# One-pass spread of the norm factors, wide-wide-low-low matmuls, and an earlier emptying of a short projection step in a fused two-block kernel

## The reference, cut to what matters

```python
def first_block(x, ...):                      # 256 tokens, D = 2048
    z = rmsnorm(x, norm_mix) @ w_in           # parts: hq hf hi hgate aq ak av g_hg g_at
    o_hg = rmsnorm(hgrn2(hq, hf, hi), hg_norm) * silu(hgate)      # 8 heads of 128
    qa, ka = rmsnorm(aq, q_norm), rmsnorm(ak, k_norm)             # heads of 64
    mixed = sigmoid(g_hg) * (o_hg @ w_hg_out) + sigmoid(g_at) * (swa_sinks(qa, ka, av) @ w_at_out)
    x = x + mixed @ w_out
    return x + square(relu(rmsnorm(x, norm_ffn) @ w_up)) @ w_down
def second_block(x, ...):
    proj = (rms_norm(x) * (1 + scale_a) + shift_a) @ w_in_2       # c drives scale, shift, gate
    diff_out = rms_norm(differential_attention(...), g_diff_sub)  # 8 heads of 128
    dsa_out = indexed_sparse_attention(...)
    x = x + gate_a * rms_norm(concat(diff_out, dsa_out) @ w_o)
    return x + gate_f * rms_norm((silu(h @ w_gate) * (h @ w_up)) @ w_down)
```

## Time and profile before

| | us |
|---|---|
| median of 3 runs | 2599.99 (2598.31 to 2602.0) |
| profiled execution, its own time | 2600.71 |
| its span in the trace | 2598.9 |
| PE busy in the span | 2545.6 (98%) |
| DVE busy | 1802.2 (69%) |
| ACT busy | 1254.9 (48%) |

### The profile page before, as it was taken

The page is one execution under the profiler, slowest core; times in us unless marked ns, Lnnn a source line. Parts: engine busy times, 40 slices in busy tenths (PEclk is TensorE's granted clock), DMA queues, the critical chain, the costliest instruction groups (busy, mean ns, idle before and its releaser), DMA issues.

```text
span 2598.9 us, 36089 instructions
## 1 busy us (share of the span) xinstructions
PE 2545.6 (98%) x14646; PEld 2214.9 (85%) x14646; DVE 1802.2 (69%) x2496; ACT 1254.9 (48%) x1868; POOL 0.2 (0%) x4
## 2 busy tenths in 40 slices
PE   7999999999999999999999999999799999999998
PEld 6888899988888888888887899987688888888886
DVE  5557547578878788788788767775766646665555
ACT  5456436455544344444444444565544444443453
POOL 0000000000000000000000000000000000000000
PEclk8999999999999999999999999999899999999999
DMA  7655444788878878879879454545477667657553
GB/s 255 199 180 169 149 146 132 248 296 280 290 237 276 295 251 309 288 259 317 277 264 326 152 178 159 151 163 183 161 240 231 224 209 227 227 192 207 185 179 129
DMA packets 349773, 574.47 MB, mean 221 GB/s; under 512 B 29414, under 2 KB 174080, under 8 KB 348712
## 3 DMA queue, kind: packets, MB, share of 16 engines
q1 hardware_dynamic: 300912, 450.53, 53.3%
q10 hardware_dynamic: 48696, 121.65, 13.4%
HBM read 560.31 MB, written 10.70 MB: 220 GB/s over the span
## 4 chain that ended last, share of the span: by engine, by line
PE 95%; DVE 2%; ACT 1%; issue 1%; DMA 0%; ACTq 0%; DVEq 0%
PE ps L453 33%; PE ps L454 17%; PE ps L476 9%; PE ps L478 9%; PE ps L477 9%; PE ps L737 3%; PE ps L957 2%; PE ps L738 2%; PE ps L739 2%; PE ps L958 2%; PE ps L959 2%; DVE wl L1702 1%; PE ps L821 1%; PE ps L542 0%; ACT wh L1031 0%
## 5 line engine op out<-in xcount | busy, mean ns | idle before, releaser
L1702 DVE TENSOR_TENSOR wl<-raw,wh 128x1024 fp32r<-128x1024 f32 x856 | 1041.1, 1224 | 749.1 <-ACT wh L1031 745.9
L1031 ACT ACTIVATE wh<-raw 128x1024 fp32r<-128x1024 f32 x856 | 900.8, 1060 | 1137.2 <-PE ps L454 555.8
L453 PE MATMUL ps<-hs,wh 128*128 128x512 f32 x3536 | 1250.3, 398 | 5.3 <-DVE hs L1888 2.9
L454 PE MATMUL ps<-hs,wl 128*128 128x256 f32 x3536 | 993.8, 281 | 0.0
L453 PEld LDWEIGHTS ps<-hs,wh 128*128 128x128 f32 x3536 | 665.2, 188 | 169.0 <-issue 3.9
L454 PEld LDWEIGHTS ps<-hs,wl 128*128 128x128 f32 x3536 | 669.4, 189 | 0.2
L476 PE MATMUL ps<-wh,ff 128*128 128x512 f32 x864 | 336.6, 390 | 0.0
L478 PE MATMUL ps<-wh,ff 128*128 128x512 f32 x864 | 336.2, 389 | 0.0
L477 PE MATMUL ps<-wl,ff 128*128 128x512 f32 x864 | 336.2, 389 | 0.0
L476 PEld LDWEIGHTS ps<-wh,ff 128*128 128x128 f32 x864 | 162.2, 188 | 33.8
L478 PEld LDWEIGHTS ps<-wh,ff 128*128 128x128 f32 x864 | 162.2, 188 | 33.7
(11 more groups left out here) (295 smaller groups left out, 2196.0 us busy)
## 6 DMA issues: line engine op xcount, KB each, us to landing
raw<-w_down SPq DMA_DIRECT2D x108, 1024.0 KB
raw<-w_in SPq DMA_DIRECT2D x80, 1024.0 KB
raw<-w_up SPq DMA_DIRECT2D x64, 1024.0 KB
ada_w<-w_ada ACTq DMA_DIRECT2D x96, 512.0 KB, 5.5
ada_more<-w_ada ACTq DMA_DIRECT2D x96, 512.0 KB, 6.5
raw<-w_gate SPq DMA_DIRECT2D x88, 512.0 KB
raw<-w_up SPq DMA_DIRECT2D x88, 512.0 KB
raw<-w_in SPq DMA_DIRECT2D x72, 512.0 KB
```

The source lines that it names most:

```text
L453: nc.tensor.matmul(ps[0:m, b, :], wh[:, slot, w0:w0 + m], x2, start=k == 0, stop=False)
L454: mm = nc.tensor.matmul(ps[0:m, b, 0:T], wl[:, slot, w0:w0 + m], x2[:, 0:T], start=False, stop=end)
L1031: nc.scalar.activation(wh[:, h % WH_SLOTS, :], raw[:, slot, HALF * q:HALF * (q + 1)], ACT.Copy).then_inc(wh_ready, 1)
L1702: nc.vector.tensor_tensor(wl[:, h % WH_SLOTS, :], raw[:, slot, HALF * q:HALF * (q + 1)], wh[:, h % WH_SLOTS, :], ALU.subtract).then_inc(wl ...
```

## The change

1. In a wide step the two pairs of a tile are written wide, wide, low, low.
2. `spread` becomes fp32r with 52 rows (rows 0 to 19 and the same again in rows 32 to 51), and the moving tile `factors` (52 x 256, fp32r) holds the high part of the factors in rows 0 to 19 and the rest in rows 32 to 51. `pair_invert` makes it with two more DVE operations, each after the one before. Since fp32r is made by an engine's write, `spread` is loaded to a side tile and copied by ACT (two copies, later one).
3. ACT and DVE empty step 10 before the `feed` of half panel 91. The first half panel of the first gate step takes its tiles in the order 2, 3, 0, 1, and waits for step 10's sums only ahead of tiles 0 and 1.
4. For PN_DIFF the squares of the last pair, its sums, the roots and the inversion move forward by one n, the spreads and the scaling from n = 101 to 100, and `attention_high` starts pair by pair; `attention_low` stands at n = 100 too.

```diff
-        spread = at("spread", [20, 20 * 64], F32, 181)
+        spread = at("spread", [52, 20 * 64], F32R, 181)
...
+        factors = at("factors", [52, T], F32R, 206)
...
                         for kk in range(2):
                             k = 2 * h + kk
-                            end = k == 4 * panels - 1
-                            x2 = rhs(n, k)
                             w0 = 512 * kk + c0
-                            nc.tensor.matmul(ps[0:m, b, :], wh[:, slot, w0:w0 + m], x2, start=k == 0, stop=False)
-                            mm = nc.tensor.matmul(ps[0:m, b, 0:T], wl[:, slot, w0:w0 + m], x2[:, 0:T],
-                                                  start=False, stop=end)
+                            nc.tensor.matmul(ps[0:m, b, :], wh[:, slot, w0:w0 + m], rhs(n, k), start=k == 0, stop=False)
+                        for kk in range(2):
+                            k = 2 * h + kk
+                            w0 = 512 * kk + c0
+                            mm = nc.tensor.matmul(ps[0:m, b, 0:T], wl[:, slot, w0:w0 + m], rhs(n, k)[:, 0:T],
+                                                  start=False, stop=k == 4 * panels - 1)
...
-                                              spread[:, c:c + P], rstd[0:20, 1, :], start=True, stop=True)
+                                              spread[:, c:c + P], factors[:], start=True, stop=True)
...
-                    for n, (c0, m) in enumerate(FULL):
+                    for n in (2, 3, 0, 1) if (s, h) == (0, 0) else range(4):
+                        c0, m = FULL[n]
                         if h == 0 and s == 0:
-                            pe.wait_ge(tile_summed, 4 * LY.step + (8 if n else 5))
+                            pe.wait_ge(tile_summed, 4 * LY.step + (5, 8, 4, 4)[n])
...
-                if n == 99:
+                if n == 98:
                     pair_sums(PN_DIFF, 4, part=PN_DIFF[3:4])
-                if n == 101:
-                    pe.wait_ge(sem("spread_loaded"), 32)
+                if n == 100:
+                    pe.wait_ge(sem("spread_loaded"), 3)
                     pair_spreads(PN_DIFF, (5, 6, 7, 4))
...
+                    if (s, h) == (10, 7):
+                        copy_halves(10, 0, 44, 0, widths=(P, P))
                     feed(8 * s + h + 4, 0)
...
+                    if (s, h) == (10, 6):
+                        act.wait_ge(sem("spread_in"), 32)
+                        for part, cols_ in spread_in:
+                            nc.scalar.activation(spread[:, cols_], part[:], ACT.Copy
+                                                 ).then_inc(sem("spread_loaded"), 1)
...
-                if n in (88, 92, 96, 98):
+                if n in (88, 92, 96, 97):
...
-                if n == 99:
+                if n == 98:
                     pair_roots(PN_DIFF, 4)
-                if n == 101:
-                    act.wait_ge(sem("pair_normed"), 13)
-                    attention_high(range(8, ND))
+                if n == 100:
+                    for j in range(4):
+                        act.wait_ge(sem("pair_normed"), 10 + j)
+                        attention_high((8 + 2 * j, 9 + 2 * j))
...
-                nc.vector.reciprocal(rstd[0:20, 1, :], rstd[0:20, 1, :]).then_inc(sem("set_inverted"), 1)
+
+                link(nc.vector.reciprocal(rstd[0:20, 1, :], rstd[0:20, 1, :]))
+                link(nc.vector.tensor_copy(factors[0:20, :], rstd[0:20, 1, :]))
+                nc.vector.tensor_tensor(factors[32:52, :], rstd[0:20, 1, :], factors[0:20, :], ALU.subtract
+                                        ).then_inc(sem("set_inverted"), 1)
...
+                    if (s, h) == (10, 7):
+                        total(10, 0, 0, z[:, Z_AK_RAW, :])
+                        total(10, 0, 1, z[:, Z_AV, :], inc=3)
                     feed(8 * s + h + 4, 0)
...
-                if n == 99:
+                if n == 98:
                     pair_invert(PN_DIFF)
-                if n == 101:
+                if n == 100:
                     pair_scale(PN_DIFF, (5, 6, 7, 4))
-                if n == 102:
-                    attention_low(range(8, 12))
-                if n == 103:
-                    attention_low(range(12, ND))
+                    attention_low(range(8, ND))
```

More of the change, by code:

```diff
@@ L168, in build @@
         sel = at("sel", [P, 2, 38], F32, 199.5)
-        spread = at("spread", [20, 20 * 64], F32, 181)
+        spread = at("spread", [52, 20 * 64], F32R, 181)
+        spread_in = [(at("spread_in0", [52, 1024], F32, 168), slice(0, 1024)),
+                     (at("spread_in1", [52, 256], F32, 122.5), slice(1024, 1280))]
+        spread_in2 = at("spread_in2", [52, 1280], F32, 156)
         psq = at("psq", [P, 2, 2, T], F32, 188)
@@ L694, in heads_of_first @@
                 if n == 0:
-                    pe.wait_ge(sem("spread_loaded"), 16)
+                    pe.wait_ge(sem("spread_loaded"), 2)
                     pair_spreads(PN_Q, (4, 5, 6, 7))
@@ L1261, in _ @@
             for s in range(6, 11):
-                halves = 8
-                for h in range(halves):
+                for h in range(8):
+                    if (s, h) == (10, 7):
+                        copy_halves(10, 0, 44, 0, widths=(P, P))
                     feed(8 * s + h + 4, 0)
@@ L1278, in _ @@
                         act.wait_ge(sem("trig_made"), 6)
-                        act.dma_start(spread[:], k_spread).then_inc(sem("spread_loaded"), 16)
+                        for part, cols_ in spread_in:
+                            act.dma_start(part[:], k_spread[:, cols_]).then_inc(sem("spread_in"), 16)
                         act.wait_ge(tile_summed, 4 * 9 + 12)
                         pair_squares(PN_Q[:2])
+                    if (s, h) == (10, 6):
+                        act.wait_ge(sem("spread_in"), 32)
+                        for part, cols_ in spread_in:
+                            nc.scalar.activation(spread[:, cols_], part[:], ACT.Copy
+                                                 ).then_inc(sem("spread_loaded"), 1)
                     if (s, h) == (10, 3):
@@ L1284, in _ @@
                         pair_roots(PN_Q, 4)
-                copy_halves(s, 0, 4 * s + 4, 0, widths=(P,) * (4 if s < 10 else 2))
+                if s < 10:
+                    copy_halves(s, 0, 4 * s + 4, 0)
             def keys_out(t0, n, count, b):
@@ L1568, in heads_of_second @@
                     act.wait_ge(sem("rope_sin"), 18)
-                    act.dma_start(spread[:], k_spread).then_inc(sem("spread_loaded"), 16)
+                    act.dma_start(spread_in2[:], k_spread).then_inc(sem("spread_in"), 16)
+                if n == 90:
+                    act.wait_ge(sem("spread_in"), 48)
+                    nc.scalar.activation(spread[:], spread_in2[:], ACT.Copy).then_inc(sem("spread_loaded"), 1)
                 if n - 7 in DIFF_UNITS:
@@ L1579, in heads_of_second @@
                     diff_values(3)
-                if n in (88, 92, 96, 98):
-                    j = (88, 92, 96, 98).index(n)
+                if n in (88, 92, 96, 97):
+                    j = (88, 92, 96, 97).index(n)
                     act.wait_ge(DIFF["out_hi"], 2 * j + 2)
@@ L2017, in _ @@
                         hg_products(h - 3)
+                    if (s, h) == (9, 0):
+                        link(nc.vector.memset(factors[:].bitcast(F32), 0.0))
                     if (s, h) == (10, 4):
                         pair_invert(PN_Q)
-                for n in range(4 if s < 10 else 2):
-                    total(s, 0, n, z[:, 4 * s + n if s < 10 else (Z_AK_RAW, Z_AV)[n], :],
-                          inc=3 if (s, n) == (10, 1) else 1)
+                if s < 10:
+                    to_z(0, s, s)
             def hg_mask(h):
@@ L2498, in constants @@
         k_dup=np.stack([(p[:, None] == 64 * h + p[None, :] % 64) for h in range(2)], axis=1).astype(f32),
-        k_sel=sel, k_spread=(np.arange(20)[:, None] == np.arange(20 * 64)[None, :] // 64).astype(f32),
+        k_sel=sel, k_spread=((np.arange(52)[:, None] % 32) == np.arange(20 * 64)[None, :] // 64).astype(f32),
         k_rot=rot, k_invf=invf, k_alibi=alibi, k_causal=causal,
```

## The result

The changed kernel took 2570.99 us (median of 4 runs, 2569.97 to 2572.05) against 2600.99 for the kernel before beside it: a ratio of 0.9882, 95% interval 0.9871 to 0.9894. The forecast was 2574 with 2561 to 2590. The profiled execution took 2572.05 us, its span is 2570.2, that is 28.7 less than the span before; the medians lie 30.0 apart.

What follows compares the result with a forecast made beforehand. PE, busy 2545.6 of 2598.9 us, was taken to set the time. Terms of 10 + 9.3 - 0.3 + 2.3 + 3.2 + 1.3 = 25.8 us off the median 2599.99 gave 2574 us, range 2561 to 2590.

Steps and rivals of the forecast that it cites:

- the order: Wide steps: wide, wide, low, low makes slow groups of four 6.6 ns shorter, quick ones unchanged; 10 us saved.
- the spreads: Spread products of PN_Q, PN_HG and PN_DIFF: 26 one-pass fp32r matmuls replace 52 records; 9.3 us saved.
- the gate start: First gate step: PE runs tiles 2 and 3 while DVE's totals are awaited; 2.3 us saved.
- The -0.3 us for the squares of PN_Q: One more DMA issue ahead of these squares may make PE wait about 0.3 us longer; bounds 0 and -0.6.
- Rival (c): Wide steps: two lows in a row leave only 0.120 us for each weight load, so slower; 2622 us, chance 0.06.
- Rival (a): Wide steps: the order makes no difference, a low beside a wide costs what it costs; 2584 us, chance 0.25.
- 26 fp32r matmuls of 256 columns at 0.120: Time of all spread products after the change: 3.1 us, against 12.0 us plus 0.4 before.
- the branch for which I had 1.6: First gate step: if the clock still falls at about 269.6 us, 1.6 us are saved, against 3.05 without a fall.
- The half clock at PN_HG: From 385.6 to 392.4 us: no clock fall expected with a block of 1 us; 3.2 us saved, bounds 0 and 3.2.
- PN_DIFF: Norm moved earlier: PE's stop ahead of L8B goes, 1.3 us saved.
- parts 2 and 5: The one-pass spread products, 9.3 us saved, and the earlier PN_DIFF removing the stop ahead of L8B, 1.3 us saved.

Runs made afterwards that it cites:

- run 3: Changed kernel with every second tile of a half panel, except in a step's first half panel, written low, low, wide, wide; 2578.54 us.
- run 9: Changed kernel in the old order, with 64 of 128 weight columns in every wide matmul of a wide step but a sum's first; 2550.49 us, one run.
- run 10: Changed kernel in the old order, with 64 weight columns in the low matmuls, all but the first and last of a sum; 2569.95 us, one run.
- run 2: Changed kernel with the old order wide, low, wide, low put back; 2584.22 us, ratio 0.9928.
- Run 7: Changed kernel with the spread matrix and the factors padded from 52 to 128 rows; 2570.99 us.
- run 11: Changed kernel once more, without further edit, to stand on one chip with a later version; 2569.57 us, ratio 0.9885.
- run 1: Kernel before with only the wide steps written wide, wide, low, low; 2589.85 us, ratio 0.9954.
- run 5: Kernel before with the moves alone (step 10 emptied first, tile order, PN_DIFF one n sooner), plain fp32 spreads, old order; 2598.3 us, ratio 0.9985.
- run 4: Kernel before with the one-pass spread alone (fp32r, 52 rows, factors in two parts); 2592.49 us, ratio 0.9965.
- run 6: Changed kernel with DVE's inversion of the PN_Q factors and ACT's two spread copies put behind the emptying of step 10; 2570.94 us.
- run 8: Changed kernel with spread padded to 128 rows, ACT's copies late, and DVE's step 10 totals ahead of the feeds of half panels 89, 90, 91; 2567.61 us, ratio 0.9869.

## Why the prediction held, point by point

The total came within 3 us of the forecast, and part of that is luck: the order brought 3.8 us more than I had, the spreads and the gate start 2.0 less. The -0.3 us for the squares of PN_Q didn't come; PE's short wait between their sums is 0.20 us before and 0.17 after.

**1. The order: the sign was right, the size 13.8 instead of 10, and the reason wrong.** I had each change of width cost the same. Run 3 has little more than half the changes and is 7.5 us slower, so that is not it. The neighbours don't cost what I took from steps of one width either: in the changed trace wide after wide takes 232.9 ns, low after low 114.6, and the two other distances 349.2 together, where I had 227, 120 and 353.3. Runs 9 and 10 show that the excess depends on the number of weight columns. That it is the loading of them, and not the writing of as many output rows, is argued: no run changes one without the other. With 64 columns in the wide, loaded while a low runs, a pair takes 0.340 us, 0.680 a group (run 9). Against that, 128 columns everywhere have an excess of 13 ns a group in the quick spacing, 27 in the slow one, and 17 in the new order. The slow spacing needs 128 columns on both sides, since it goes when either is halved (one execution each). The new order never shows it; for that it gives up the quick one, 0.697 against 0.693. So slow groups gained 10 ns, not 6.6, and quick ones lost 3.3, where I had them unchanged. 0.79 x 1896 x 10 - 0.21 x 1896 x 3.3 is 13.7 us, and the trace has 13.8. Rival (c), too little room in a row of lows, was refused for two lows by this result. For four, run 3 shows its size, 4 ns a group: a low takes 118.3 ns there in the mean and 115.3 in the changed kernel, and the wides no more than before.

The Trainium skill, TensorE: Matmul & The Clock Gate, section "LDWEIGHTS (loading the stationary operand)", gives a load of P columns P / 1.2 ns, that is 107 ns for 128 columns and 53 for 64. At the 2.4 GHz of the same page a stream of 256 columns takes 107 ns too; that is an estimate. So a low would only just cover a full load, and a wide would cover it with ease. Run 9 agrees with this; run 10 does not, since a shorter load under the wide should have changed nothing and took away the slow spacing.

The Trainium skill, TensorE: Matmul & The Clock Gate, section "Back-to-back issue gap", says that in a stream of weight loads and matmuls both set the distance between matmuls. Runs 9 and 10 agree in kind; its figure for 512 columns, 131 ns, is not what the across steps show, 227. Rival (a), that the order makes no difference, had the changed kernel at 2584 us; it came out at 2571, and the same kernel in the old order (run 2) at 2584.

What stays open is why the old order has two spacings, and what puts a stretch into one of them. It isn't the kind of spread (run 2), and it differs between runs of one kernel.

**2. The spreads: 9.3 us forecast, 7.9 measured.** The count and the 3.65 us were right. The step that was off is "26 fp32r matmuls of 256 columns at 0.120": a block of eight takes 1.14 and a block of two 0.43, 3.85 us in all instead of 3.1. The longer distance behind a block stays (0.4 us in all), and 0.25 went to the half clock at the first block. Run 7 names the reason, the 52 rows of weights between matmuls of 128; I had written that the rows change nothing that the trace shows, which was so only because no row of before had a one-pass matmul of few rows. DVE's two operations took 0.28 and 0.41 us, and from the first of them to the `feed` behind them it takes 0.76, against 0.9.

**3. The gate start: 2.3 us forecast, 1.7 measured.** The stop was 2.00 us against 2.05, in the place forecast, and the clock fell: the branch for which I had 1.6. A stop of 1.9 to 2.1 us stands there in seven traces: behind it the clock fell in four (the changed kernel and runs 2, 9 and 10) and not in three (3, 7 and 11). Behind the stop near 616 us it fell in the traces of before and of runs 1, 3, 6 and 9 and not in the others. A single execution has the one or the other, so taking the middle was fair, and what decides stays open.

**4. The half clock at PN_HG: 3.2 us forecast, 3.1 measured.** The kernel before and runs 1 and 5 have plain fp32 spreads and all show it; the changed kernel and the ten other runs have one-pass spreads and none does. I had written that it depended on where the block came, because the same block at the two other places was followed by no fall. That was wrong: in run 5 the clock fell at both. So the long block brings the fall on here in three traces of three and at each of the two other places in one of three; why not always stays open.

**5. PN_DIFF: 1.3 us forecast, 1.5 measured.** The sum was right and the split between parts 2 and 5 was not: run 4 shows that without the move the shorter block would have gained nothing here, the stop growing by 2.5 us. The two are one edit. The `feed`s behind the split were ready in time.

What the forecast didn't have: 1.4 us at the clock near 628 us, and -1.0 in the first step, both of kinds that differ from run to run; no experiment isolates them.

## What to carry to other kernels

When every matmul loads its own weights, look at which load falls under which stream, and read the distances of every order from a trace: the order of the same instructions decided here between 0.693, 0.697, 0.701 and 0.707 us a group. Longer runs of one kind are not better without end; two and two was the best that came in every run, four and four was worse. When an engine has several things to do while another waits, ask of each for when it is needed; moving one of them only moved the stop (run 6), and letting those wait that nobody needed yet removed it (run 8).

## What the runs showed of the hardware that I had not expected

- The same instructions, wide and low in turn, run at 0.3467 or 0.3533 us a pair in stretches of up to hundreds of us, and this makes kernels of that order scatter by some 10 us from run to run. Wide, wide, low, low ran at 0.697 a group in each of seven traces, and its times scattered by 3 us at most.
- A matmul of 512 columns among its like takes 226.7 ns only some time after narrower ones. At the start of an across step, behind the lows of a wide step, the first 2 to 10 distances are nearly all between 228 and 241 ns. It looks as if loads that fell behind were caught up slowly; that is argued from distances, no run isolates it.
- A block of one-pass matmuls with 52 rows of weights among others of 128 rows makes four distances longer by 0.09 to 0.1 us each: the one before it, its first, its last and the one behind it. With 128 rows, zeros included, none is longer.
- A block of 20-row fp32 matmuls, 3.65 us long at full clock, ran into 6.8 us at half clock at PN_HG in all three traces that had it. At the two other places it ran into 3.4 us at half clock in one trace (run 5) and into none in two. Behind the one-pass block at PN_HG there was none in eleven traces.
